# The value product of an RWKV-7 layer as three products of rounded parts, with its weights in chunks of half the rows

## What is computed

```
h  = rms_norm(x, norm_g)
dx = token_shift(h) - h
x_r, x_w, x_k, x_v, x_a, x_g = (h + dx * mu[i] for i in range(6))
r = x_r @ w_in[:, c[0]:c[1]]          # each 512x1024 @ 1024x1024
k = x_k @ w_in[:, c[1]:c[2]]
v = x_v @ w_in[:, c[2]:c[3]]
g = silu(x_g @ w_in[:, c[3]:c[4]])
w_lo = tanh(x_w @ w_in[:, c[4]:c[5]]); a_lo = x_a @ w_in[:, c[5]:c[6]]
log_decay = -exp(-softplus(-(w0 + w_lo @ w_up)) - 0.5)
a = sigmoid(a0 + a_lo @ a_up)
# kk = k * k_k, normalised by head; k = k * (1 + (a - 1) * k_a)
# scan over the 512 positions, for each of 16 heads of width 64:
S = S * w_t + (S @ -kk_t) (kk_t * a_t)^T + v_t k_t^T;  y_t = S @ r_t
# group norm of y, the bonus sum(r * k * r_k) * v, times g, then @ w_out
```

## Time and profile before

| | us |
|---|---|
| median of 3 runs | 796.61 |
| lowest, highest | 793.84, 796.99 |
| the profiled execution, its own time | 794.85 |
| its span, first to last instruction | 793.0 |
| PE busy in it | 754.0 (95%) |
| DVE busy | 442.4 (56%) |
| ACT busy | 306.3 (39%) |
| POOL busy | 171.2 (22%) |
| mean granted clock of TensorE | 0.985 |

### The profile page before, as it was taken

One profiled execution on the slowest core, in us unless ns is written; L12 is line 12 of the kernel. 1 busy time (PEld: TensorE's weight loads), 2 busy tenths in 40 slices (PEclk: granted clock), 3 DMA queues, 4 the chain that ended last, 5 costly groups with the idle time before them and its releaser, 6 DMA issues.

```text
span 793.0 us, 17638 instructions
## 1 busy us (share of the span) xinstructions
PE 754.0 (95%) x7612; PEld 610.9 (77%) x7612; DVE 442.4 (56%) x799; ACT 306.3 (39%) x637; POOL 171.2 (22%) x132
## 2 busy tenths in 40 slices
PE   3999999999999998988899999999999999999997
PEld 3488888777787777778788888877777777775797
DVE  5952624777998233346755415679636766743511
ACT  5534444566622122233442356233234444333200
POOL 1244430000143312324211002910000000004542
PEclk9999999999999889899999999999999999999999
DMA  8032225224176864330005037023102111231131
GB/s 252 28 107 86 77 77 160 80 80 95 51 175 151 214 221 139 110 108 5 3 3 212 1 108 177 27 80 107 54 27 68 40 54 54 67 107 53 55 107 54
DMA packets 116766, 72.83 MB, mean 92 GB/s; under 512 B 26833, under 2 KB 114129, under 8 KB 116689
## 3 DMA queue, kind: packets, MB, share of 16 engines
q1 hardware_dynamic: 98496, 65.12, 27.8%
q10 hardware_dynamic: 18192, 6.58, 3.5%
HBM read 64.35 MB, written 7.34 MB: 90 GB/s over the span
## 4 chain that ended last, share of the span: by engine, by line
PE 83%; DVE 9%; DMA 3%; issue 3%; ACT 1%; SPq 1%; POOLq 0%; POOL 0%; ACTq 0%; DVEq 0%
PE bank L522 20%; PE bank L991 9%; PE bank L516 6%; PE bank L518 6%; PE bank L517 6%; DVE arena L1621 3%; PE bank L1032 2%; PE bank L1015 2%; PE bank L635 2%; PE bank L770 2%; PE bank L541 2%; PE bank L684 2%; PE bank L1111 2%; PE bank L1113 2%; PE bank L1112 2%
## 5 line engine op out<-in xcount | busy, mean ns | idle before, releaser
L522 PE MATMUL bank<-arena 128*128 128x256 f32 (+1 forms) x768 | 180.7, 393 | 1.4 <-DVE arena L1878 1.4
L522 PEld LDWEIGHTS bank<-arena 128*128 128x128 f32 x768 | 144.5, 191 | 35.0 <-issue 17.1
L2001 POOL TENSOR_TENSOR w_lo<-arena,w_hi 128x1024 fp32r<-128x1024 f32 x24 | 58.5, 2439 | 185.6 <-ACT w_hi L1203 185.6
L1203 ACT ACTIVATE w_hi<-arena 128x1024 fp32r<-128x1024 f32 x44 | 46.4, 1057 | 93.3 <-DMA arena<-w_in 77.7
L516 PE MATMUL bank<-x_hi,w_hi 128*128 128x512 f32 x192 | 76.6, 399 | 0.0
L518 PE MATMUL bank<-x_hi,w_lo 128*128 128x512 f32 x192 | 75.6, 393 | 0.0
L517 PE MATMUL bank<-x_lo,w_hi 128*128 128x512 f32 x192 | 75.3, 392 | 0.0
L516 PEld LDWEIGHTS bank<-x_hi,w_hi 128*128 128x128 f32 x192 | 36.1, 188 | 9.0 <-issue 1.2
L2097 POOL COPY arena<-arena 128x512 f32<-128x512 f32 x4 | 2.5, 615 | 185.7 <-DVE arena L1911 185.7
L518 PEld LDWEIGHTS bank<-x_hi,w_lo 128*128 128x128 f32 x192 | 36.0, 188 | 8.3
L517 PEld LDWEIGHTS bank<-x_lo,w_hi 128*128 128x128 f32 x192 | 36.1, 188 | 7.9
(11 more groups left out here) (249 smaller groups left out, 1605.2 us busy)
## 6 DMA issues: line engine op xcount, KB each, us to landing
arena<-w_in SPq DMA_DIRECT2D x45, 512.0 KB, 3.9
arena<-w_ada SPq DMA_DIRECT2D x12, 1024.0 KB, 5.4
arena<-w_in SPq DMA_DIRECT2D x8, 1024.0 KB, 5.5
arena<-w_out SPq DMA_DIRECT2D x8, 1024.0 KB, 5.1
lt_dram<-arena ACTq DMA_DIRECT2D x16, 256.0 KB, 2.3
arena<-x SPq DMA_DIRECT2D x4, 512.0 KB, 5.6
arena<-x SPq DMA_DIRECT2D x1, 2048.0 KB, 7.5
out<-arena SPq DMA_DIRECT2D x8, 256.0 KB, 2.1
```

Of the source, the lines that this page charges most:

```text
L522: last = mm(o, lhs(k), rhs(k), start=(k == 0), stop=(k == n - 1))
L1203: A(WHI[n % 3][:, :], WR[n % 3][:, 0:1024], ACT.Copy).then_inc(weights_rounded, 1)
L2001: TT(WLO[n % 3][:, :], WR[n % 3][:, 0:1024], WHI[n % 3][:, :].bitcast(f32), SUB)\
```

## The change

The value product is taken as three products of rounded parts too. Its weights come as eight chunks of 256 columns and half the rows (k = 0 to 3, then 4 to 7; 512 KB each) in place of four blocks; all are now in `SPLIT_A`, so ACT rounds and POOL splits each. `value_rows(c)` uses chunk c for all four position tiles, 48 products of 128x256, so that two bank pairs are open over two iterations (`VALUE_BANKS`), and ACT copies both halves of a finished block at odd c. Mixture 4 is rounded by ACT and split by DVE in the r stage, in memory that the k mixture has left; mixture 5's rounding and splitting move from the value loop to the r stage. In the value loop ACT rounds chunk c+2 (for c = 6 and 7 the gate's first two blocks) at the end of each iteration. `first_l` now always takes banks 2 and 3, the up-projections 0 and 1, and the first gate product bank 3. Parts 0 and 1 of `solve(0)`, whose memory now holds the mixture, move behind the value loop. ACT stores the second inverse after its take of gate 5 rather than of gate 4. SP's numbers 43 and 46 become 47 and 50, the same places in the stream.

```diff
@@ -217,9 +217,10 @@
         XHI, XLO = [{m: [rounded(f"{n}{m}_{c}", at + c * T, T) for c in range(KT)] for m, at in places}
-                    for n, places in (("x_hi", ((2, b0 + 4096), (3, ab_at), (5, ht_at))),
-                                      ("x_lo", ((2, b0 + 8192), (3, v_at), (5, b0))))]
+                    for n, places in (("x_hi", ((2, b0 + 4096), (3, ab_at), (4, b0 + 8192), (5, ht_at))),
+                                      ("x_lo", ((2, b0 + 8192), (3, v_at), (4, b0 + 4096), (5, b0))))]
         WMU = KB[:, 6:8, :].rearrange("p c t -> p (c t)").rearrange("p (k n) -> p k n", k=KT)
+        nth_mix = {2: 0, 3: 1, 4: 2, 5: 3}
         nth_split = {2: 0, 3: 1, 5: 2}
@@ -342,6 +343,7 @@
         k_inverse, k_spread = sem("k_inverse"), sem("k_spread")
+        v_rounded, v_mixed, v_chunk = sem("v_rounded"), sem("v_mixed"), sem("v_chunk")
         x_summed, x_rooted, dx_ready, low_scaled = [sem(n) for n in ("x_summed", "x_rooted", "dx_ready", "low_scaled")]
@@ -382,7 +384,9 @@
             stream += [cols(w_in, first + P * b, P) for b in range(KT)]
-        stream += [cols(w_in, 2 * D + 256 * b, 256) for b in range(4)]
+        w_in_rows = w_in.rearrange("(k p) n -> p k n", p=P)
+        stream += [(w_in_rows[:, 4 * r:4 * r + 4, 2 * D + 256 * b:2 * D + 256 * b + 256], 4, 256) for b in range(4)
+                   for r in range(2)]
         split_g = len(stream)
@@ -395,7 +399,7 @@
-        SPLIT_A = list(range(1, 1 + 2 * KT)) + list(range(split_g, split_g + KT))
+        SPLIT_A = list(range(1, split_g + KT))
         SPLIT_D = list(range(split_d, split_d + 8)) + list(range(split_d + 9, split_d + 21))
@@ -589,7 +593,7 @@
                 pe.wait_ge(ab_ready, c + 1)
-                o = [next_bank(("lt", c, h)) for h in range(2)]
+                o = [out_bank(("lt", c, h), 2 + h) for h in range(2)]
                 for j in range(NT):
@@ -598,29 +602,49 @@
+            VALUE_BANKS = [(4, 5), (6, 4), (5, 6), (4, 5)]
+
+            def value_rows(c):
+
+                b, r = divmod(c, 2)
+                lo, hi = split_weights()
+                for h in range(2):
+                    if r == 0:
+                        out_bank(("v", b, h), VALUE_BANKS[b][h])
+                    o = banks[VALUE_BANKS[b][h]]
+                    for i in range(2):
+                        oi, at = o[:, i * 256:(i + 1) * 256], slice((2 * h + i) * P, (2 * h + i + 1) * P)
+                        for k in range(4):
+                            kx, wk = 4 * r + k, slice(k * 256, (k + 1) * 256)
+                            if c < 2 and h == 0 and i == 0:
+                                pe.wait_ge(v_mixed, kx + 1)
+                            mm(oi, XHI[4][kx][:, at], hi[:, wk], start=(r == 0 and i == 0 and k == 0), stop=False,
+                               skip_group_check=True)
+                            mm(oi, XLO[4][kx][:, at], hi[:, wk], start=False, stop=False, skip_group_check=True)
+                            last = mm(oi, XHI[4][kx][:, at], lo[:, wk], start=False, stop=(r == 1 and k == 3),
+                                      skip_group_check=True)
+                        if c and h == 0 and i == 0:
+                            bonus(c - 1)
+                    if r == 1:
+                        full(last, ("v", b, h))
+                if r == 0:
+                    last.then_inc(v_chunk, 1)
+                    block_key[taken[0] - 1] = ("chunk", b + 1)
+
             for c in range(KT):
-                o = [next_bank((name, c)) for name in ("w", "a")]
+                o = [out_bank((name, c), i) for i, name in enumerate(("w", "a"))]
                 for s, name in ((0, "w"), (1, "a")):
...
                         .then_inc(bank_full[where[name, c][0]], 1)
-                if c % 2 == 0:
-                    w = weights()
-                pe.wait_ge(mixed, KT * 3)
-                b, h = divmod(c, 2)
-                o = next_bank(("v", b, h))
-                for i in range(2):
-                    t = 2 * h + i
-                    last = accumulate(o[:, i * 256:(i + 1) * 256], lambda k: XI[0][:, k, t * P:(t + 1) * P],
-                                      lambda k: w[:, k, :])
-                    if c and i == 0:
-                        bonus(c - 1)
-                full(last, ("v", b, h))
+                value_rows(c)
                 if c == 0:
...
             first_l(KT - 1)
+            turn[0] = 2
+
@@ -813,7 +837,7 @@
                     if c == 0:
-                        pe.wait_ge(mixed, KT * 3 + k + 1)
+                        pe.wait_ge(mixed, KT * 2 + k + 1)
                     last = split_product(o, lo, hi, XLO[5][k][:, :], XHI[5][k][:, :], k)
@@ -1139,18 +1163,20 @@
                         sp.wait_ge(mods_block, key)
+                    elif key[0] == "chunk":
+                        sp.wait_ge(v_chunk, key[1])
                     else:
...
                     sp.dma_start(UPS[side[1], :], a_up).then_inc(ups_here, 16)
-                if n == 43:
+                if n == 47:
                     sp.wait_ge(y_made, GROUPS)
...
                     sp.dma_start(CX, ctx_x.rearrange("(t p) n -> p t n", p=P)).then_inc(ctx_here, 16)
-                if n == 46:
+                if n == 50:
                     sp.dma_start(NEAR, near).then_inc(rel_here, 16)
@@ -1203,8 +1229,8 @@
             def round_mix(m, c):
-                act.wait_ge(mix_rough, KT * nth_split[m] + c + 1)
-                A(XHI[m][c][:, :], MIXES[m][:, c, :], ACT.Copy).then_inc(mix_rounded, 1)
+                act.wait_ge(mix_rough, KT * nth_mix[m] + c + 1)
+                A(XHI[m][c][:, :], MIXES[m][:, c, :], ACT.Copy).then_inc(v_rounded if m == 4 else mix_rounded, 1)
@@ -1240,13 +1266,16 @@
                     square_k(c + 1)
-                if c + 10 < 2 * KT:
-                    round_weights(c + 10)
+                round_mix(4, c)
+                round_weights(c + 10)
                 if c:
...
                 free(A(KINV[c % 2], arrived(act, ("kss", c))[:, 0:2 * NT], ACT.Sqrt), ("kss", c))
+                if c:
+                    round_mix(5, c - 1)
             spread_norm(KT - 1)
+            round_mix(5, KT - 1)
             def copy_l(c):
@@ -1287,20 +1316,19 @@
                 A(MID[:, NE:2 * NE], MID[:, 0:NE], ACT.Exp, scale=-KAPPA).then_inc(decays_ready, 1)
-                b, h = divmod(c, 2)
-                o = arrived(act, ("v", b, h))
-                vh = VC[side[1 - b // 2], 4 * h:4 * h + 4, b % 2 * 256:b % 2 * 256 + 256]
-                for s in range(2):
-                    ins = A(vh.rearrange("p (i s) n -> p i s n", s=2)[:, :, s, :],
-                            o[side[s], :].rearrange("p (i n) -> p i n", i=2), ACT.Copy)
-                free(ins, ("v", b, h))
-                round_mix(5, c)
+                b = c // 2
+                for h in range(2 * (c % 2)):
+                    o = arrived(act, ("v", b, h))
+                    vh = VC[side[1 - b // 2], 4 * h:4 * h + 4, b % 2 * 256:b % 2 * 256 + 256]
+                    for s in range(2):
+                        ins = A(vh.rearrange("p (i s) n -> p i s n", s=2)[:, :, s, :],
+                                o[side[s], :].rearrange("p (i n) -> p i n", i=2), ACT.Copy)
+                    free(ins, ("v", b, h))
                 if c in (4, 5):
...
                     copy_l(c - 1)
-                if c >= 6:
-                    round_weights(2 * KT + c - 6)
+                round_weights(2 * KT + c + 2)
             copy_l(KT - 1)
@@ -1310,12 +1338,12 @@
                 if c + 2 < KT:
-                    round_weights(2 * KT + c + 2)
+                    round_weights(3 * KT + c + 2)
                 take_gate(c)
...
                         fetch_blocks(q)
-                if c in (1, 4):
+                if c in (1, 5):
                     store_inverse(c // 4)
@@ -1563,8 +1591,9 @@
-                dve.wait_ge(mix_rounded, KT * nth_split[m] + c + 1)
-                TT(XLO[m][c][:, :], MIXES[m][:, c, :], XHI[m][c][:, :].bitcast(f32), SUB).then_inc(mixed, 1)
+                dve.wait_ge(*((v_rounded, c + 1) if m == 4 else (mix_rounded, KT * nth_split[m] + c + 1)))
+                TT(XLO[m][c][:, :], MIXES[m][:, c, :], XHI[m][c][:, :].bitcast(f32), SUB)\
+                    .then_inc(v_mixed if m == 4 else mixed, 1)
@@ -1598,8 +1627,11 @@
                 mix(5, c)
+                split_mix(4, c)
                 if c:
                     norm_k(c - 1)
+                    split_mix(5, c - 1)
+            split_mix(5, KT - 1)
@@ -1625,8 +1657,6 @@
             for c in range(KT):
-                if c >= 6:
-                    solve(0, c - 6)
                 stored(dve, ("w", c))
@@ -1653,14 +1683,13 @@
                     norm_k(KT - 1)
-                split_mix(5, c)
             arrived(dve, ("v", 3, 1))
...
             free(nc.vector.tensor_copy(BON, arrived(dve, "bonus")[:, 0:64]), "bonus")
-            for part in range(2, 5):
+            for part in range(5):
                 solve(0, part)
```

(5 more changed lines are left out.)

## The result

| | before | after |
|---|---|---|
| median of the runs, us | 795.69 (4 runs, 793.84 to 796.99) | 804.60 (4 runs, 801.91 to 805.22) |
| profiled execution, its time / its span | 794.85 / 793.0 | 804.38 / 802.6 |
| mean granted clock | 0.985 | 0.973 |

The ratio is 1.0103, with a 95% interval from 1.0062 to 1.0143: 8 us slower, and slower than half a per cent with fair certainty. The forecast was 801.5 and its range 791 to 806.

What follows compares the result with a forecast made beforehand. PE bounded the old value loop; ACT, with DVE's wait inside it, would bound the new one. DVE's path at +6.0 and PE's at +6.4 were taken as +6.2 on 794.85, giving 801.1; forecast 801.5, range 791 to 806.

Steps and rivals of the forecast that it cites:

- PE's own work: Value loop: rounded products at 0.119 us each cut PE's iteration to 8.7 us and take 12.7 us from PE.
- ACT and DVE as the new bound: Value loop: DVE's step blocked by POOL's split, ACT waiting for DVE; two iterations take 21.15 us, formerly 20.6.
- PE's waits before the bonus: Value loop: PE idle ahead of the bonus product, by 1 and 3 us in turn.
- The loop's end: End of value loop: tanh of iteration 7 at 207.3, DVE ending the loop where it did, at 216.7.
- DVE's path: Value loop's end to second modulation product, through the second inverse, its store, fetches and w_ada: +6.0 us.
- The seventh split: Gate stage: one more POOL split falls among the inverses' steps on DVE, +1.9 us.
- the two paths: DVE's and PE's chains after the loop, meeting at the second modulation product; they agree at about +6.2 us.
- Store, fetches and w_ada follow unchanged: After the second inverse: its store, SP's fetches and the w_ada block keep their times, leaving DVE's path at +6.0 us.
- PE's path: Gate stage: first gate product waits for copy_l(7), starting 6.6 us later; with absorbed wait and clock term, +6.4 us.
- the uncertain term: Gate stage's start: PE at half clock after idling, between 0 and 4.4 us, 1.4 taken.
- The sum: Whole kernel: +6.2 us on the profiled 794.85 gives 801.1; predicted 801.5; +4 to +8 given chance 0.47.
- the first (PE sets the pace, 787.9): Value loop: DVE gets past POOL's split, PE sets the pace; -7 us, 787.9; chance 0.14.

Runs made afterwards that it cites:

- e2_less_pe: Changed kernel with only the product of the rounded parts in the value sum, the two low-part products left out: 807.37 us, 1.0125 of before.
- e1_dve_split: Changed kernel with the seven splits in the value loop made by DVE at the end of its iteration instead of POOL: 797.10 us, 0.9994 of before.
- e7_store_gate4: Changed kernel with the second inverse's store put back behind gate 4 on ACT: 801.28 us, 1.0048 of before.
- e3_hold_ada: Changed kernel with SP issuing the first w_ada block only once the second inverse's store has landed: 802.90 us, 1.0077 of before.
- e4_banks: Changed kernel with last first_l and gate products in other banks, so neither waits for copy_l(6) or copy_l(7): 801.68 us, 1.0071 of before.
- e8_dve_all: Changed kernel with loop and gate splits on DVE, e4_banks' banks, second w_ada block before second inverse's fetches, first inverse's store one gate later: 786.29 us, 0.9860 of before.
- e12_two_ahead: e10_late_split with the third w_ada block, too, ahead of the second inverse's fetches on SP: 788.00 us, 0.9873 of before.
- e10_late_split: e8_dve_all with DVE's loop split moved behind the centred sums that ACT's exponentials wait for: 787.18 us, 0.9893 of before.
- e9_act_fetch: e8_dve_all with the second inverse's eight fetches issued by ACT behind gate 6 instead of by SP: 801.04 us, 1.0057 of before.

## Why the prediction was right, and where it was off

- **PE's own work** (12.7 us less): the spacing was 0.119 us as read from the earlier trace rows, but the sum was too large. An iteration without waits takes PE 9.11 us, bonus to bonus, and not 8.7; before it took 10.28 (175.99 to 186.27). Where one kind of product follows another the step is 0.21 to 0.23 us and not 0.12, four times in an iteration, and the sum had no term for it. So eight iterations give back 9.4 us. The forecast doesn't hang on this term: e2_less_pe shows that less work of PE's brings nothing in this order.
- **ACT and DVE as the new bound:** right, and close in its numbers. L1661 2.1 us, tanh to exponential 5.1, steps of 9.5 and 11.7 (measured 9.4 to 9.7 and 11.9 to 12.3). Off were PE's waits before the bonus, forecast at 1 and 3 us in turn: they were 0, 0, 1.89, 0, 0.39, 0.54, 2.65 and 1.19 us. PE, longer at its own work than forecast and at half clock behind the longer waits, used part of that room. e1_dve_split shows the cause by taking it away.
- **The loop's end:** the tanh of iteration 7 forecast at 207.3, measured 207.81; iterations 1, 2 at 141.1 and 155.4, measured 140.78 and 155.22; DVE's last step of the loop ends at 217.2 (216.7).
- **DVE's path:** forecast +6.0 at the second inverse, measured +7.5. The seventh split came as forecast (L1657 2.57 us instead of 0.64; without it the inverse is done 2.3 us earlier in e7_store_gate4). But two of the seven ran largely beside waits and cost DVE only 0.3 and 1.2 us, so that all seven cost 10.9 us where six had cost 10.8. What was missing are those waits, 0.82 us at gate 1 and, above all, 1.72 us at 243.79: DVE stood at gate 2, because ACT's tanh of it stood behind a rounding whose weights had come late, since the gate stage had started late. The forecast had the two paths side by side and not this crossing between them. Parts 0 and 1 took 6.3 us, from 217.43 to 223.75, of which 2.1 are a split beside them: the 4.1 us forecast, as the profile shows them, though no run tried them by themselves: their working space holds the rounded mixture of the values until the loop's end.
- **"Store, fetches and w_ada follow unchanged":** this is the step that failed. It was +4.5 us: the store 8.70 instead of 5.14, the fetches 7.00 instead of 6.04. The earlier trace rows held for a `w_ada` block that had been issued 2.5 us ahead of the store; in the new order it was issued 1 us ahead. The block took 6.7 us to land here and 5.8 before, so both were in flight together for 5.7 us where it had been 3.3. The prediction looked at the order on SP alone, not at its times against ACT's store. e3_hold_ada, e4_banks and e7_store_gate4, each in its way, bring the store back to 3.9, 2.9 and 3.5 us. Why the fetches took 1 us more stays open: the block had landed before they were issued.
- **PE's path:** the gate stage forecast at 222.7, measured 222.67, released by `copy_l` as said. That the clock would be at half was the uncertain term (0 to 4.4 us, 1.4 taken); the first ten products ran at half for 4.4 us, so it cost about 2. The clock fell at about 217.5, within the wait of 2.46 us ahead of the last `first_l`, and was still at half when the gate stage began. The Trainium skill (TensorE: Matmul & The Clock Gate, HAM oscillation) had said that a gap between bursts sends the engine back to half clock; the trace now agrees, behind 1.89 us of idle time in the loop and within those 2.46 us, gaps shorter than those of the page's example. PE's last gate product ended 7.0 us later (+6.4 forecast).
- **The sum:** +6.2 forecast. By the two paths' meeting it was +12.0, by the end of the profiled execution +9.5, by the ratio +8.2. The profile shows where part came back: a stretch of half clock that lay at 720 to 740 us before (0.91 there) is not there after (1.00), some 1.7 us. The prediction had read the clock as low in the scan only and missed that stretch; that it was gone is luck, and it brought the time nearer to the forecast. That both paths came to +6.2 in the prediction was a coincidence too: at its end DVE's was the later by far.
- **The rivals:** the first (PE sets the pace, 787.9) names what e1_dve_split made true, and its own sum was too good: 797.1. It had counted the split as free once DVE gets past it, and PE's pair of iterations as 17.4 us, where it is 18.2. With the gate stage's splits out of the way as well the kernel does reach 786.3.

So mechanism and sign were right. The size, forecast as +4 to +8 us, came out at its upper edge, and in the path itself well above it. The largest reason is that a transfer was priced from its row without asking what would be in flight beside it.

## What to carry to other kernels

Work taken from the busiest engine is worth what its neighbours leave of it: before PE's work is cut in half its cost, ask which instruction the new helper work will run beside. A split that POOL did for nothing beside an idle DVE cost 1.7 us each time in the loop, and DVE did the same split for 1.2 in its own queue. And a transfer's duration belongs to what is in flight with it: when a change shifts one queue by some microseconds against another, price the transfers on both anew.

## What the hardware showed that was not expected

- Beside a POOL step with SBUF operands, DVE's steps split into two kinds. With all operands in SBUF, a TENSOR_SCALAR, a TENSOR_TENSOR, a SCALAR_TENSOR_TENSOR and a COPY waited for its end (0.43 us became 2.13, 0.51 became 2.39, 0.68 became 2.88 at 141.00 in the changed kernel, 0.64 became 2.57). Steps that read a PSUM bank didn't (SCALAR_TENSOR_TENSOR 0.69 and TENSOR_TENSOR 1.28 for two, in e7_store_gate4 beside the split of 261.07), nor did memsets, nor a TENSOR_REDUCE of 128x200 in SBUF (0.36 beside the split of 247.39 in the same run). It goes the other way too: POOL's 1.28 us became 2.00 where DVE's step was first. The Trainium skill (SBUF — State Buffer, Who interferes with whom) draws this line: steps with two inputs in SBUF contend, and so can copies and tensor_scalar, which have a mode that takes both ports, while reductions never do; and the order of issue decides who blocks. The rows agree.
- Behind a wait of 1.89 us in a loop that is otherwise dense PE's clock was at 0.50 for 6.6 us, and behind one of 2.65 us for 3.2. Those of 0.39 and 0.54 us at 183.89 and 193.60 left it at 1.00, and so did one of 1.01 us at 180.40 in e1_dve_split.
- A DMA issue holds the engine that makes it, the longer the more is in flight: eight 64 KB fetches took 6.0 to 7.0 us on SP with no other block in flight (before, e4_banks, after), 9.3 to 9.4 with a 1 MB block issued just ahead of them (e3_hold_ada, e8_dve_all), 10.2 with two (e12_two_ahead), and 14.1 on ACT with SP's blocks beside them.
- The 512 KB store took 3.9 us with no 1 MB block beside it (e3_hold_ada) and 3.5 with one issued 2.2 us behind it (e7_store_gate4). With the block ahead it took 2.9 us at 4.5 us ahead (e4_banks), 5.14 at 2.5 (before), 6.3 at 1.5 (e8_dve_all), 8.6 and 8.70 at 1.1 and 1.0 (e2_less_pe, after), but 7.15, 6.8 and 4.8 at 0.4 to 0.5 (e10_late_split, e9_act_fetch, e12_two_ahead). So the distance matters and is not all; what else does isn't shown.
